# State space input projection: first half of the rows taken for both column blocks first, with one block's partial sums parked in SBUF

## What is computed

```python
mod = c_act @ ada_w[i] + ada_b[i]            # 2048 x 12288 for each layer
sh1, sc1, g1, sh2, sc2, g2 = [m[:, None, :] for m in jnp.split(mod, 6, axis=-1)]
h = x * (1.0 + sc1) + sh1
u = h @ in_w                                  # 2048 x 2048, the projection
bu = jnp.einsum('gnp,blgp->lbgn', b_bar, ug)  # then a scan over the tokens
```

## Time and profile before

| | before |
|---|---|
| median of 3 runs | 2490.12 us (2487.67 to 2490.86) |
| the profiled execution's own time | 2485.89 us |
| its span, first to last instruction | 2484.2 us |
| PE busy | 96% of the span |
| DVE busy | 75% |
| ACT busy | 42% |
| mean DMA rate | 253 GB/s |
| product 0 of the projection starts | 93.67 us |
| the last product of the projection ends | 207.3 us |

### The profile page before, as it was taken

One profiled execution on the slowest core, in us unless ns is written; L12 is line 12 of the kernel. 1 busy time (PEld: TensorE's weight loads), 2 busy tenths in 40 slices (PEclk: granted clock), 3 DMA queues, 4 the chain that ended last, 5 costly groups with the idle time before them and its releaser, 6 DMA issues.

```text
span 2484.2 us, 33024 instructions
## 1 busy us (share of the span) xinstructions
PE 2394.9 (96%) x12457; PEld 1924.3 (77%) x12457; DVE 1853.9 (75%) x2964; ACT 1045.8 (42%) x1242; POOL 35.3 (1%) x67
## 2 busy tenths in 40 slices
PE   5799799999999999999999999999999999999998
PEld 3377468878888888888878888778888888888886
DVE  6377979977778887889878987887777755455457
ACT  4254024464443444344464444464544344434442
POOL 0000000000000000000000000000000000000000
PEclk9899899999999999999999999999999999999999
DMA  9996938858888998899758877736788666656674
GB/s 308 361 334 229 393 114 291 300 186 295 301 276 300 345 319 271 276 331 313 250 164 301 280 252 231 223 102 195 229 299 294 229 193 188 189 188 199 188 219 144
DMA packets 314686, 627.36 MB, mean 253 GB/s; under 512 B 30656, under 2 KB 31072, under 8 KB 314272
## 3 DMA queue, kind: packets, MB, share of 16 engines
q1 hardware_dynamic: 310240, 611.35, 73.5%
q0 software_dynamic: 4288, 13.90, 2.0%
HBM read 623.05 MB, written 2.10 MB: 252 GB/s over the span
## 4 chain that ended last, share of the span: by engine, by line
PE 85%; DVE 9%; DMA 3%; ACT 2%; issue 1%; SPq 0%; DVEq 0%; ACTq 0%
PE psB L2112 40%; PE psA L2112 39%; DVE prod L1424 2%; DMA col_raw<-in_ada_w 1%; PE psT L1707 1%; DVE tmp L1429 1%; DVE st L1435 1%; PE psM L1739 1%; PE psA L1947 1%; DVE w_lo L1103 1%; DMA Cnat_im<-in_s_c_im 0%; DMA w_raw<-in_dsa_out_w 0%; DVE ada_acc L1120 0%; DVE w_lo_more L1103 0%; DMA w_raw<-in_s_glu_w 0%
## 5 line engine op out<-in xcount | busy, mean ns | idle before, releaser
L1103 DVE TENSOR_TENSOR w_lo<-w_raw,w_hi 128x1024 fp32r<-128x1024 f32 x732 | 893.0, 1223 | 487.0 <-ACT w_hi L784 482.6
L784 ACT ACTIVATE w_hi<-w_raw 128x1024 fp32r<-128x1024 f32 x732 | 774.8, 1060 | 1110.0 <-PE psB L2112 483.6
L2112 PE MATMUL psB<-w_hi,hT_hi 128*128 128x512 f32 x1040 | 407.0, 391 | 0.6 <-DVE w_lo L1103 0.6
L2112 PE MATMUL psB<-w_hi,hT_lo 128*128 128x512 f32 x1040 | 404.9, 389 | 0.0
L2112 PE MATMUL psB<-w_lo,hT_hi 128*128 128x512 f32 x1040 | 404.7, 389 | 0.0
L2112 PE MATMUL psA<-w_hi,hT_hi 128*128 128x512 f32 x1008 | 397.9, 395 | 5.1 <-DVE w_lo L1103 2.0
L2112 PE MATMUL psA<-w_hi,hT_lo 128*128 128x512 f32 x1008 | 393.2, 390 | 0.0
L2112 PE MATMUL psA<-w_lo,hT_hi 128*128 128x512 f32 x1008 | 392.9, 390 | 0.0
L1120 DVE SCALAR_TENSOR_TENSOR ada_acc<-ada_raw,csil,ada_acc 128x512 f32<-128x512 f32 x450 | 336.1, 747 | 13.2 <-DVE ada_acc L1120 0.5
L2112 PEld LDWEIGHTS psB<-w_hi,hT_hi 128*128 128x128 f32 x1040 | 195.2, 188 | 44.7 <-issue 2.8
L2112 PEld LDWEIGHTS psA<-w_hi,hT_hi 128*128 128x128 f32 x1008 | 189.6, 188 | 49.5 <-issue 8.0
(11 more groups left out here) (368 smaller groups left out, 2330.0 us busy)
## 6 DMA issues: line engine op xcount, KB each, us to landing
w_raw<-in_ffn_w_in SPq DMA_DIRECT2D x352, 512.0 KB, 4.6
ada_raw<-in_ada_w SPq DMA_DIRECT2D x480, 256.0 KB, 5.4
w_raw<-in_ffn_w_out SPq DMA_DIRECT2D x176, 512.0 KB, 4.5
col_raw<-in_ada_w SPq DMA_DIRECT2D x128, 512.0 KB, 6.2
w_raw<-in_dsa_in_w SPq DMA_DIRECT2D x112, 512.0 KB, 4.8
w_raw<-in_s_glu_w SPq DMA_DIRECT2D x56, 512.0 KB, 5.7
w_raw<-in_s_in_w SPq DMA_DIRECT2D x32, 512.0 KB, 6.7
w_raw<-in_dsa_out_w SPq DMA_DIRECT2D x32, 512.0 KB, 5.4
```

Source lines behind the costliest of these rows:

```text
L784: nc.scalar.activation(high(u), w_raw[:, u % RING], ACT.Copy).then_inc(w_hi_ready, 1)
L1103: V.tensor_tensor(low(u), w_raw[:, u % RING], high(u).bitcast(F32), ALU.subtract).then_inc(w_lo_ready, 1)
L2112: ins = MM(PS[s][:, t, 0:r.width], a_[:, kt, tok], b_[:, kk, 0:r.width], start=kt == 0 and m == 0, stop=k == r.units - 1 and kk == UK - 1 ...
```

## The change

`MIXED` goes from 48 to 40 column units; the other 24 stand between the first products as 12 pairs. The projection has a new order, `placed`: block 1 with k = 0 to 3 (8 products), whose sums ACT copies to a new tile `partial` in SBUF; then block 0 with k = 0 to 3 and 4 to 7; then block 1 with k = 4 to 7, to which DVE adds `partial` (this copy from PSUM was ACT's before). `partial` takes the place of half of the early units' ring, which so has 6 slots in place of 8, two of them in a region that also holds the tiles `staged` of `make_h`: early unit 4 waits for `h_ready`, the end of h. The early units are spread over iterations 16 to 27 in place of 10 to 27. The 16 diagonals on ACT are made in two lots of 8.

```diff
-MIXED = FRONT - AU
+MIXED = FRONT - 24
...
-        early_raw = [at("early_raw0", "growA", [P, 4, AW]), at("early_raw1", "more", [P, 4, AW])]
+        early_raw = [at("early_raw0", "growA", [P, 4, AW]), at("early_raw1", "uT", [P, 2, AW], plus=8 * K)]
+        partial = at("partial", "more", [P, 2, TOK, NB])
...
-        s5_in = Run("u", 2, s5_in_w[0], (0, NB), dense=(0, EARLY, 4, 10), before="x")
+        s5_in = Run("u", 2, s5_in_w[0], (0, NB), dense=(0, EARLY, 4, 16), before="x")
...
-        beside = (4, 4, 4, 2, 2, 0, 0, 0)
-        crossed = [(k, s) for k in range(6) for s in range(2)] + [(6, 0), (7, 0), (6, 1), (7, 1)]
+        beside = (0, 2, 2, 2, 2, 2, 2, 2, 2, 2, 2, 2, 2, 0, 0, 0)
+        closing_early = [(0, 0), (0, 1), (1, 0), (1, 1), (2, 0), (3, 0), (2, 1), (3, 1)]
+        placed = [(1, k, s) for k, s in closing_early]
+        placed += [(0, k, s) for k in range(4) for s in range(2)]
+        placed += [(0, k + 4, s) for k, s in closing_early]
+        placed += [(1, k, s) for s in range(2) for k in range(4, 8)]
...
-                if u >= ARING:
-                    sp.wait_ge(ada_used, u - ARING + 1)
+                ring = 6 if q < EARLY else ARING
+                if u == 4:
+                    sp.wait_ge(h_ready, s5_in.h0 + 4)
+                if u >= ring:
+                    sp.wait_ge(ada_used, u - ring + 1)
...
+                if n >= 2:
+                    for q_, k in ada_units(s5_in, 0, n - 2):
+                        if q_ + k == 0:
+                            sp.wait_ge(col_used, FRONT)
+                        ada_unit(q_, k)
...
-                            sp.wait_ge(ada_used, EARLY * AU - ARING // 2)
+                            sp.wait_ge(ada_used, EARLY * AU)
+                        elif m == 6:
+                            sp.wait_ge(T_full, s5_in.turn + 3)
...
-            def skip_diagonals():
-
-                act.wait_ge(ada_used, EARLY * AU)
-                for f in range(KT):
+            def skip_diagonals(s):
+
+                act.wait_ge(part_added, s + 1)
+                for f in range(8 * s, 8 * s + 8):
...
+                    for n in range(len(placed)):
+                        if n in (6, 8):
+                            act.wait_ge(w_used, n)
+                            s = (n - 6) // 2
+                            nc.scalar.activation(partial[:, s], PS[s][:], ACT.Copy).then_inc(part_free[s], 1)
+                        if n in (product(r, 0, 0), product(r, 0, 1)):
+                            finish(r, 0, n // product(r, 0, 1))
+                        hi_to(n, 2, filled_to(r))
+                        if n == 13:
+                            read_row(1)
+                        if n in (14, 15):
+                            make_h(n - 12)
+                            h_high(n - 12)
+                        if n in (25, 27, 31):
+                            turned(r, *((0, 0), (0, 1), (1, 0))[(n - 25) // 2 if n < 31 else 2])
+                        if n == 30:
+                            skip_diagonals(0)
...
+                if r.kind == "u" and i == 1:
+                    vec.wait_ge(w_used, product(r, i, s))
+                    vec.wait_ge(T_full, r.turn + s + 1)
+                    vec.wait_ge(part_free[s], 1)
+                    V.tensor_tensor(stg[s][:], PS[s][:], partial[:, s], ALU.add).then_inc(ps_free[s], 1)
```

More of the change, by code:

```diff
@@ L560, in product @@
         def product(r, i, s):
-            if r is s5_in and i + s == 0:
-                return r.unit + crossed.index((r.units - 1, 0)) + 1
+            if r is s5_in:
+                return placed.index((i, r.units - 1, s)) + 1
             return r.unit + i * r.per + (s + 1) * r.units
@@ L664, in _ @@
                             sp.wait_ge(col_used, glu_after(n - r.units))
-                        elif u >= 8:
+                        else:
                             sp.wait_ge(w_lo_ready, rounded(u - RING))
-                        if u >= 8 and not whole(r, i, n // r.units):
+                        if not whole(r, i, n // r.units):
                             w_unit(r, i, n)
@@ L1651, in _ @@
                     h_low(0)
+                    vec.wait_ge(scaled_turned, 8)
+                    lo_unit(0)
                     h_low(1)
[L1653 to L1657, removed]
+                    for n in range(len(placed)):
+                        if n == product(r, 1, 0):
+                            finish(r, 1, 0)
+                        lo_to(n, 2, filled_to(r))
+                        if n == 14:
                             front_columns(1)
-                        if n in (5, 7):
-                            h_low((n - 1) // 2)
+                        if n in (15, 16):
+                            h_low(n - 13)
                         for c, kk in ada_units(r, 0, n):
                             ada_unit(c, kk)
-                for i in range(r is s5_in, r.n):
+                        for c in ada_ended(r, 0, n, 4):
+                            store_chunk(c)
+                for i in range(r.n if r is not s5_in else 0):
                     u = r.unit + i * r.per
@@ L2104, in operands, with products @@
                 return hT_hi, hT_lo
-            def products(r, s, k, t, u, hi, lo):
+            def products(r, s, k, t, u, hi, lo, begin=0, end=None):
                 tok = slice(t * P, (t + 1) * P)
@@ L2150, in _ @@
                 if r is s5_in:
-                    crossing()
+                    projection()
                 elif r.before == "s5":
@@ L2167, in _ @@
                             turn_keys()
-                        if r is s5_in and n == 1:
-                            turn(r, 0, 0)
                         if s == 1 and k == 3:
```

81 lines of the change are left out of this document (42 added, 39 removed).

## The result

The changed kernel takes **2510.76 us** (median of 4 runs, 2508.90 to 2511.96) beside 2488.89 us for the kernel before on the same chip (4 runs, 2487.51 to 2490.86): ratio 1.0087, 95% interval 1.0069 to 1.0104, **21.9 us slower**. The forecast was slower, 2502.5 in a range of 2483 to 2513. So direction and range held, and the loss is some three quarters larger than the 12.4 us of the sum.

The account below looks back on a forecast made before the run. The prediction took column loads, then PE, to bound the projection, and DVE's recurrence after it. Projection end +10.8 and end of block +1.6 gave +12.4 us: 2485.9 became 2498.3, and 4.2 more for the median 2502.5, range 2483 to 2513.

Parts of the forecast that it names:

- The start: First products of the projection: weight unit 0 issued earlier, product 0 at about 85.6, some 8 us earlier.
- The mixed part: Products 2 to 13, each with a pair of column units: 3.9 us a step, 43 us for eleven steps.
- Copies to `partial`: Two ACT copies of 1.03 us, covered by ACT's 55.3 us of waiting; without the cover they would cost 2.
- The turn to the second half of h: Products 14 to 16: waits for the row and later parts of h give back some 5 us; product 16 near 151.
- The loop: Products 20 to 31: early-unit uses, loads and splits close over two iterations, 9.3 us, 4.65 a step; product 31 ends at 218.
- one for one: Behind the projection: what moves its end moves the rest of the kernel by the same time; nothing absorbs it.
- The end: Behind the last product: DVE's add of `partial` +0.3 and the second lot of diagonals +1.3, together +1.6 us.
- (a): Products 20 to 31: the loop holds, the step as priced within 0.6 us; 2496 to 2510 us, chance 0.50.
- (d): Products 2 to 13 run at before's pace, 4.55 us a step, adding 7 to 8 us: 2510 us, chance 0.12.
- (e): Products 20 to 31: PE's clock falls in the loop, adding 8 us: 2511 us, chance 0.08.
- (b): Products 20 to 31: loop shorter than the transfers, which set the pace; kernel near 2482 us, chance 0.18.
- (c): Products 20 to 31: in between, loop near 7.5 us and no change that can be told, chance 0.12.

Follow-up runs that it names:

- experiment 1: The changed kernel with 4 slots in place of 6 for the early units: 2545.20 us, ratio 1.0223 to the kernel before.
- experiment 2: The changed kernel with every early unit one iteration later in the SP queue: 2489.35 us, ratio 1.0004 to the kernel before.
- experiment 3: The kernel before with only the early units changed, to 6 slots and iterations 16 to 27: 2506.27 us, ratio 1.0069.
- experiment 5: experiment 2 with five smaller waits taken away by moving work on ACT and DVE, the second diagonals behind ACT's last copy of states: 2499.94 us.
- experiment 9: experiment 5 with the second lot of diagonals back where the changed kernel has it, ahead of ACT's copies of states: 2483.19 us, ratio 0.9979.
- experiment 11: The changed kernel with 26 of 32 early loads left out and later quarters of h formed ahead of the weight unit's split: 2488.67 us.

## Why the prediction was right in sign and short in size

**The start** was right: product 0 at 85.21, predicted 85.6. Products 0 and 1 then took 5.3 and 5.2 us to the next one, at a granted clock of 0.54 between 84 and 91 us, near the lower level, where I had allowed some 3.7 each, and product 2 came at 95.62 in place of 93: 2.6 us late.

**The mixed part** was predicted at 3.9 a step and 43 us; it took 46.9. Ten of the eleven steps took 3.92 to 4.38. One took 6.13, and here a step of the working failed: "Copies to `partial` ... are covered by the 55.3 us in which ACT waited". ACT is in order, and the copy stood behind a split that waited 2.89 us for its load; product 9 waited 2.1 us for the copy, the 2 us that the prediction had for copies "without the cover". A sum of idle time covers nothing if the wait stands ahead of the work in the same queue. So product 13 was at 142.56 and not 136, and the change was worth 8.2 us there and not "some 16" (136 would have been 14.8 ahead of the 150.79 before): only the head start.

**The turn to the second half of h** was right: products 13 to 16 took 13.7 us against 8.2 before, 5.5 given back, predicted 5. The prediction's own times, 136 and 151, have 15 us here, so 1.3 us of the late start were made good.

**The loop** was right as a mechanism (experiments 1 to 3) and as a size for a lap: 9.3 to 9.7 predicted, 9.36 measured after a first lap of 10.57. Two terms in it offset each other a little: the landings on the chain in the four laps took 6.09, 5.15, 4.51 and 4.19, 5.0 in the mean where I took 4.7, and the hand-overs, taken as 0.1 each without a row, show as 0.02 to 0.05. Its two ends were off. It began late: SP went on at 160.80 where I had 156, since h was late with product 13, and product 20 was at 169.51, not 163. And it ended late: product 31 came 56.2 us behind product 20, 5.1 a step, not 51. The last landing took 6.79 us with column loads behind it in place of 4.7, product 30 waited 2.1 for the second chunk's sum, and ran 1.7 us longer at the lower clock. So the last product ended at 228.7 and not at 218, and against the kernel before it was 21.4 us late where the sum has 10.8. That term of the sum is the one that was mis-sized, and 6.5 of its error of 10.7 us lie ahead of the loop and not in it. The last product ended 21.4 us late and the recurrence's last step 22.8, so "one for one" held here; experiment 5, with its projection done earlier and its time longer, shows that it isn't the whole path.

**The end** was right in size: from the end of the last product to the recurrence's first step 12.2 us against 11.0 before, +1.2, predicted +1.6. Experiments 5 and 9 show that not the 2.4 us of diagonals but their place in the order is what can cost.

**The rivals.** (a) had the mechanism, and the step of 5.1 lies within 0.6 of its 4.65, but the result is 0.8 us above its 2496 to 2510. That (d) and (e) named 2510 and 2511, nearer to the result, was chance: neither was the cause. (b), that the transfers set the pace, is excluded by a DMA share of 0.72 to 0.83 in the loop, and (c), with its lap of 7.5, by the laps. (d), 4.55 a step in the mixed part, was too high, 4.27 with the one wait. (e), the clock in the loop: the Trainium skill's "TensorE: Matmul & The Clock Gate", section "HAM oscillation", has the clock drop and the transition paid for every tile. The granted clock did drop, to 0.80 to 0.89, but products that wait for a load hide it, and about 1.7 us show on the chain. Of landings, the Trainium skill's "DMA: Bandwidth & Descriptors", section "Anatomy of one DMA", would have given an estimate of 3.4 us for 512 KB; that section fits loads issued from GpSimd, and these come from SP. The loads of weight units in the loop's chain took 4.19 to 6.79 here, so the measured rows were the better price.

**What stays open**: how much the wait of early unit 4 for h costs in the changed kernel by itself (its trace shows 2.13 us of PE's wait at product 20 behind it; experiment 11 didn't resolve the rest), what the smaller ring and the later start cost one without the other, and which of the three waits that experiments 5 and 9 take away together (the copy, the row, the quarters of h) gave most of the 6 us between experiments 2 and 9. In the two traces the step behind product 8 is 2.0 us shorter (4.38 for 6.41, the copy), and products 12 to 16 take 3.1 us less (15.5 for 18.5, the row and the quarters).

## What to carry to other kernels

When a ring gets fewer slots, or its use is pressed into fewer iterations, count how many whole iterations back the slot's last use lies, and divide: (issue + landing + every engine step up to that use) over that number is the pace of everything in the same in-order queue. If it is above the work's own step, either keep the slots or put the loads that may wait behind those that may not; here one position in the queue was worth 21 us, more than the whole rearrangement gained.

Idle time of an engine is cover only if the added work stands where the idleness is, not behind the instruction that waits. That holds for work put later as much as for work added: eight small copies moved to a place that looked free cost some 15 us.

## What was not expected of the hardware

TensorE stayed at half of its clock while it was fully busy. In experiment 5 the granted clock was 1.00 from 218 to 225 us; after a gap of 4.47 us it was 0.50 in two stretches in which PE was busy 14.00 of 14 us, with matmuls of 64 columns and column-unit matmuls (weights of 128x32, 512 columns). In experiment 9, where the same work came without the gap, it was 1.00 up to 246 us, and fell only after that (0.75, then 0.62), when PE was busy 7.87 and 8.90 of 14 us:

```profile
225.00:232.00 7.00, 7.00 (x66) 4.98 (x69) 5.26 (x36) 6.48 (x7) 0.00 (x0) 1.00 0.70 243
232.00:246.00 14.00, 13.28 (x108) 7.86 (x100) 14.00 (x91) 0.47 (x1) 0.00 (x0) 1.00 0.99 365
```

The landing of a load of 256 KB in the changed kernel, whose SP queue stood still between the laps, was as short as 2.5 us, where the shortest before was 4.6:

```profile
L605 SPq DMA_DIRECT2D early_raw<-in_ada_w x32: 327/328/808, 145.6 to 208.4; - x32
...
DMA to landing us min/median/max: 2.5/4.2/7.6
```
